# Mixing stages of a two-block network: rotation and turned blocks under the projection, gates by exponential and reciprocal

## The reference

```python
proj = n @ w_in                     # n: (256, 1024), normalised and modulated
# columns: NSA q, kv, gates (12); dilated q,k,v (6 heads); forgetting q,k,v (6 heads), f (6); merge gates (3*1024)
y_a = nsa(rope(q_a), rope(kc), vc, rope(ks), vs, rope(kw), vw, nsa_g, ...)   # compressed + 2 windows, 4 heads
# dilated: three groups of two heads; every group's own softmax and log-sum-exp
p, lse = masked_softmax(q k^T * scale);  out_g = p @ v
y_b = sum_g softmax_g(lse)[g] * out_g
# forgetting: cum = cumsum(log_sigmoid(f + bias)); scores + cum_q - cum_k, causal softmax
y_c = forgetting(fq, fk, fv, ...)
g_a, g_b, g_c = split(sigmoid(merge_g), 3)
merged = g_a * (y_a @ br_nsa) + g_b * (y_b @ br_dil) + g_c * (y_c @ br_fox)
h = h + gate * (merged @ w_out)
```

## Time and profile before

| | |
|---|---|
| runs (3) | median 2143.99 us, 2140.99 to 2145.86 |
| profiled execution | 2144.57 us, its span 2142.8 us |
| mean granted TensorE clock | 0.949 of full |
| busy: PE / DVE / ACT / POOL | 1964.4 / 1377.5 / 997.1 / 82.3 us |
| HBM read | 455.43 MB, 213 GB/s over the span |

### The profile page before, as it was taken

The page is one execution under the profiler, slowest core; times in us unless marked ns, Lnnn a source line. Parts: engine busy times, 40 slices in busy tenths (PEclk is TensorE's granted clock), DMA queues, the critical chain, the costliest instruction groups (busy, mean ns, idle before and its releaser), DMA issues.

```text
span 2142.8 us, 29870 instructions
## 1 busy us (share of the span) xinstructions
PE 1964.4 (92%) x12658; PEld 1746.6 (82%) x12658; DVE 1377.5 (64%) x1467; ACT 997.1 (47%) x1161; POOL 82.3 (4%) x105
## 2 busy tenths in 40 slices
PE   7999879999997999997997899999999879879998
PEld 3977668888885999896875799989998877768997
DVE  4888558999995777664335587777755443355444
ACT  3344337777774433443444433343334434435342
POOL 1320000000001000000000000000001000000000
PEclk9988979999998999997998999999999989989999
DMA  8655328999994687553321387658753432124554
GB/s 347 238 210 185 156 109 334 367 357 350 349 376 173 256 299 262 224 217 107 109 79 71 146 325 293 266 190 335 292 185 139 176 118 79 67 91 158 178 194 149
DMA packets 63877, 458.42 MB, mean 214 GB/s; under 512 B 7040, under 2 KB 7296, under 8 KB 8832
## 3 DMA queue, kind: packets, MB, share of 16 engines
q1 hardware_dynamic: 63744, 456.51, 56.7%
HBM read 455.43 MB, written 1.05 MB: 213 GB/s over the span
## 4 chain that ended last, share of the span: by engine, by line
issue 80%; PE 7%; DVE 6%; DMA 3%; ACT 2%; POOL 1%; DVEq 1%; POOLq 0%; ACTq 0%; SPq 0%
DMA ada<-in_ada 2%; DVE acc L326 2%; PE PS L353 2%; PE PS L354 2%; PE PS L355 1%; DVE wlo L280 1%; PE PS L1194 1%; POOL Z L485 1%; ACT whi L274 1%; DVE hlo L462 1%; PE PS L1258 1%; DMA raw<-in_stream 0%; ACT Z L441 0%; PE PS L1270 0%; DVE sm L1702 0%
## 5 line engine op out<-in xcount | busy, mean ns | idle before, releaser
L280 DVE TENSOR_TENSOR wlo<-raw,whi 128x2048 fp32r<-128x2048 f32 x282 | 646.6, 2294 | 409.1 <-ACT whi L274 403.6
L274 ACT ACTIVATE whi<-raw 128x2048 fp32r<-128x2048 f32 x282 | 538.5, 1913 | 408.4 <-PE PS L355 364.1
L353 PE MATMUL PS<-whi,hhi 128*128 128x256 f32 (+1 forms) x1616 | 530.2, 328 | 39.7 <-DVE wlo L280 11.7
L354 PE MATMUL PS<-wlo,hhi 128*128 128x256 f32 (+1 forms) x1616 | 518.5, 321 | 0.0
L355 PE MATMUL PS<-whi,hlo 128*128 128x256 f32 (+1 forms) x1616 | 518.0, 321 | 0.0
L353 PEld LDWEIGHTS PS<-whi,hhi 128*128 128x128 f32 x1616 | 319.9, 198 | 65.8 <-issue 13.7
L355 PEld LDWEIGHTS PS<-whi,hlo 128*128 128x128 f32 x1616 | 319.6, 198 | 19.2
L354 PEld LDWEIGHTS PS<-wlo,hhi 128*128 128x128 f32 x1616 | 320.3, 198 | 17.6
L353 PE MATMUL PS<-hhi,whi 128*128 128x256 f32 x1152 | 326.6, 284 | 2.2 <-DVE mod L348 2.2
L355 PE MATMUL PS<-hhi,wlo 128*128 128x256 f32 x1152 | 326.0, 283 | 0.0
L354 PE MATMUL PS<-hlo,whi 128*128 128x256 f32 x1152 | 326.0, 283 | 0.0
(11 more groups left out here) (377 smaller groups left out, 1822.0 us busy)
## 6 DMA issues: line engine op xcount, KB each, us to landing
raw<-in_stream SPq DMA_DIRECT2D x285, 1024.0 KB, 4.8
ada<-in_ada SPq DMA_DIRECT2D x92, 1024.0 KB, 4.9
ada<-in_stream SPq DMA_DIRECT2D x48, 1024.0 KB, 4.9
raw<-in_ada SPq DMA_DIRECT2D x3, 1024.0 KB, 15.5
xs<-in_x SPq DMA_DIRECT2D x1, 1024.0 KB, 11.7
Z<-in_ada SPq DMA_DIRECT2D x1, 1024.0 KB, 19.4
Z<-in_ctx SPq DMA_DIRECT2D x1, 1024.0 KB, 11.8
masks<-in_masks SPq DMA_DIRECT2D x2, 512.0 KB, 9.6
```

Of the source, the lines that this page charges most:

```text
L274: nc.scalar.activation(whi[:, s], src, ACT.Copy).then_inc(hi_ready, 1)
L280: nc.vector.tensor_tensor(wlo[:, s], src, whi[:, s].bitcast(F32), ALU.subtract).then_inc(lo_ready, 1)
L353: nc.tensor.matmul(out_, ah, bh, start=start, stop=False, skip_group_check=check)
L354: nc.tensor.matmul(out_, ah, bl, start=False, stop=False, skip_group_check=check)
```

## The change

Layer by layer in the mixing stage:

- Unit 11 of the projection (forget and NSA gate columns) streams and is projected first (`QKV_ORDER`). The forget logarithm starts on VectorE after unit 2 and ends after unit 4, the rotation follows after unit 5. The turned blocks go, in a new order with block 10 first, between projection units 7 to 11 (`TURNS_AT`).
- The running sums follow gate 0, their turns gate 1, and the compression gate 2. `oc_out` moves ahead of one `conv_lo`.
- The weights of the dilated groups come from row maxima and row sums: exp(m - max m) * sum instead of exp of m + ln(sum). They and the results of the dilated and first forgetting heads are made between the last maxima.
- Gates: sigmoid(x) becomes 1 / (1 + exp(-x)); the exponential on ScalarE (for gates 4 to 11 within the eviction), the addition and the reciprocal on VectorE (`gate_sigmoid`), between maxima of the passes; gate 11 after the passes.
- Results are turned in pairs of blocks as they become ready, beside gate 11; the third branch and the merged sum are handled in quarters. The products of the branches use other PSUM banks.

The diff, cut (`...` marks what is left out):

```diff
+QKV_ORDER = [11] + list(range(11))
+TURNS_AT = {7: (0, 4), 8: (4, 8), 9: (8, 12), 10: (12, 16), 11: (16, 17)}
...
-        ORDER2 = list(range(11, 17)) + list(range(11))
+        ORDER2 = [10, 8, 9, 6, 7, 0, 1, 2, 3, 4, 5] + list(range(11, 17))
...
-        ATT_GATES = {3 * (h // 2) + h % 2: (5 + h // 2, h % 2) for h in range(14)}
+        ATT_GATES = {3 * (h // 2) + h % 2: (5 + h // 2, h % 2) for h in range(12)}
...
             for j in range(3, 12):
                 pe.wait_ge(*B["q_out"].at(j - 3, l))
                 project(unit(pe, QK0 + j, E0), hhi, hlo, QB[j % 3]).then_inc(unit_used, 1)
...
+                if j == 7:
+                    pe.wait_ge(*B["rope2"].at(0, l))
+                    pe.wait_ge(*N2.row.at(1, l))
+                if j in TURNS_AT:
+                    pe.wait_ge(*B["q_out"].at(j - 1, l))
+                    turn_blocks(*TURNS_AT[j])
...
+                if i == PASSES2:
+                    pe.wait_ge(*B["y2_made"].at(0, l))
+                    turn_two(xn, 0, 6)
+            pe.wait_ge(*B["y2_made"].at(1, l))
+            turn_two(xn, 2, 4)
+            pe.wait_ge(*B["m_out"].at(10, l))
+            gate_unit(11, 7, 0)
+            pe.wait_ge(*B["y2_made"].at(2, l))
+            turn_two(xn, 4, 5)
+            gate_unit(11, 7, 1)
...
+                if f < 4:
+                    ins = nc.scalar.activation(G[f], src, ACT.Copy)
+                else:
+                    ins = nc.scalar.activation(G[f], src, ACT.Exp, scale=-1.0)
...
+                    if i < 4:
+                        nc.scalar.activation(G[i], G[i], ACT.Exp, scale=-1.0).then_inc(*B["gate_exp"].up)
...
-            for b in range(3):
-                for f in range(4 * b, 4 * b + 4):
-                    ins = nc.scalar.activation(G[f], G[f], ACT.Sigmoid)
-                ins.then_inc(*B["sig_done"].up)
...
             for j in range(12):
                 conv_lo(dve, QK0 + j + RING, E0)
+                if j == 2:
+                    fox_start()
+                if j == 4:
+                    fox_log()
+                if j == 5:
+                    rotate()
                 if l == 0 and 1 <= j <= 8:
...
+                if j in TURNS_AT:
+                    turned_out(*TURNS_AT[j])
...
+            def gate_sigmoid(f):
+                dve.wait_ge(*(B["gate_exp"] if f < 4 else B["m_out"]).at(f, l))
+                nc.vector.tensor_scalar(G[f], G[f], 1.0, None, ALU.add)
+                dve.drain()
+                nc.vector.reciprocal(G[f], G[f])
...
             for i in range(PASSES2):
                 dve.wait_ge(*B["s2_mm"].at(i, l))
...
                 if done[1]:
                     conv_lo(dve, CG[done[0]] + RING, E0)
+                    gate_sigmoid(done[0])
+                if i < 5:
+                    gate_sigmoid(i)
+                if i == 15:
+                    dil_weights()
+                if i == 18:
+                    dil_out()
+                if i == 19:
+                    fox_out(14, 2, 4, 256)
+            fox_out(16, 4, 5, 0)
```

More of the change, by code:

```diff
@@ L1837, in gate_unit, with turn_two @@
                     ins.then_inc(unit_used, 1)
-            gate_unit(0, 4)
[L1840 to L1853, removed]
+            pe.wait_ge(*B["tb_act"].at(7, l))
+            def turn_two(src, c0, bank):
+                for c in range(2):
+                    for t in range(NT):
+                        o = c * 256 + t * P
+                        ins = nc.tensor.transpose(PS[:, bank, o:o + P], src[:, t, (c0 + c) * P:(c0 + c + 1) * P], ident)
+                ins.then_inc(*B["y2_turned"].up)
+            gate_unit(0, 4)
             pe.wait_ge(*B["tb_dve"].at(7, l))
@@ L1955, in pe_layer @@
             pe.wait_ge(*B["br_out"].at(0, l))
[L1956 removed]
+            rows_product(u, 1, yb_hi[:, 3], yb_lo[:, 3], 0, True, False).then_inc(unit_used, 1)
             u = unit(pe, BR0 + 2, E0)
[L1958 to L1962, removed]
+            rows_product(u, 0, yb_hi[:, 4], yb_lo[:, 4], 0, False, False)
@@ new lines, in pe_layer @@
+            wh, wl = (w.rearrange("p (k n) -> p k n", k=2)[:, 1] for w in u)
+            for half in range(2):
+                for t in range(NT):
+                    o, w = slice(t * P, (t + 1) * P), slice(half * 512, half * 512 + 512)
+                    ins = mm3(PS[:, 2 * t + half], yb_hi[:, 5, o], yb_lo[:, 5, o], wh[:, w], wl[:, w], False, True)
+                ins.then_inc(*(unit_used, 1) if half else B["dil_mm"].up)
+            for j in range(4):
+                pe.wait_ge(*B["br_out"].at(2 + j, l))
+                turn_two(mg, 2 * j, 4 + j)
@@ L2287, in dve_layer @@
             dve.wait_ge(unit_used, E0 * 3 + (BR0 + 1))
-            branch(0, 4, mg)
+            for j in range(4):
+                ins = gated(0, j, 0, mg)
+            ins.then_inc(*B["br_out"].up)
             conv_lo(dve, BR0 + RING, E0)
             dve.wait_ge(*B["dil_mm"].at(0, l))
-            branch(1, 0, mt2[0])
-            conv_lo(dve, BR0 + 1 + RING, E0)
-            dve.wait_ge(unit_used, E0 * 3 + (BR0 + 3))
-            branch(2, 4, mt2[1])
-            conv_lo(dve, BR0 + 2 + RING, E0)
@@ L2296, in dve_layer, with merged @@
-            split_dve(dve, B["y2_hi"], B["y2_lo"], 3, 4, l)
+            for j in range(4):
+                gated(1, j, 4, mt2[0])
+            dve.drain()
+            nc.vector.tensor_tensor(mg, mg, mt2[0], ALU.add).then_inc(*B["br_out"].up)
+            dve.wait_ge(*B["dil_mm"].at(1, l))
+            def merged(j):
+                c = slice(256 * j, 256 * j + 256)
+                nc.vector.tensor_tensor(mg[:, :, c], mg[:, :, c], mt2[1][:, :, c], ALU.add).then_inc(*B["br_out"].up)
+            for j in range(2):
+                for t in range(NT):
+                    c = slice(256 * j, 256 * j + 256)
+                    nc.vector.tensor_tensor(mt2[1][:, t, c], PS[:, 2 * t, c], G[8 + j][:, t], ALU.mult)
@@ L2297, in dve_layer @@
+            dve.drain()
+            merged(0)
+            dve.wait_ge(unit_used, E0 * 3 + (BR0 + 3))
+            gated(2, 2, 0, mt2[1])
+            merged(1)
+            gated(2, 3, 0, mt2[1])
+            dve.drain()
+            merged(2)
+            merged(3)
+            for j in range(4):
+                split_lo(3 + j, 4 + j, hhi[:, 2 * j:2 * j + 2], hlo[:, 2 * j:2 * j + 2])
+            for u in range(1, 3):
+                conv_lo(dve, BR0 + u + RING, E0)
             conv_lo(dve, WO0 + RING, E0)
@@ L2510 @@
         gates = list(wide(m[:, fq + 1158:]))
-        seq += ffn[0] + list(wide(qkv)) + gates[:3] + [w1[:, :UNIT], w1[:, UNIT:]] + gates[3:]
+        seq += ffn[0] + [wide(qkv)[u] for u in QKV_ORDER] + gates[:3] + [w1[:, :UNIT], w1[:, UNIT:]] + gates[3:]
         seq += list(tall(branches)) + list(tall(a["mix_w_out_2"][l])) + ffn[1]
```

282 lines of the change are left out of this document (158 added, 124 removed).

## The result

The changed kernel takes 2155.8 us (median of 5 runs, 2153.5 to 2159.6), the kernel before beside it 2143.95 (5 runs, 2141.0 to 2145.9). The ratio is 1.0055, with a 95% interval of 1.0041 to 1.0070: slower by 0.55%, about 12 us. The prediction was 2156.

A forecast was written before the change was run, and what follows sets the result against it. TensorE, busy for 92% of the span, was taken as the bound, with VectorE's queue ahead of the maxima delaying it. Layer 0 at +9.6 and layer 1 at +1.5 made +11 on 2144.6, about 2156 us, range 2134 to 2182.

The forecast's parts named there:

- projection, layer 0: QKV projection of layer 0: 4.1 us of moved transposes, 4.9 of waits (rope2 2.9, evicted block 2.0), 3.4 of clock.
- front: Last projection unit to first attention mask: 42.5 us instead of 69.6, with no wait over 1.1 us left.
- attention: The 20 attention passes: 100.1 us grows by 26.4 from VectorE's queue and 8.5 from the clock, to 135.0.
- tail: Last attention pass to output projection: 32.5 us, a gain of 10.6 per layer, with gate 11 moved there.
- (3): Rival: a reciprocal takes 4.3 us, adding 22 us at 11 places per layer, 2178 us in all; chance 0.14.
- (4): Rival: long reciprocals stream better; about 2127 us at 2.0 us each, 2105 at the addition's cost; chance 0.16.
- the 22: Attention: each microsecond of reciprocal price changes the kernel's time by 22 us, from 11 places per layer on the path.
- the clock's 17 us: Attention, both layers: low clock behind TensorE's holes, charged at 1.7 us after each of five, 8.5 per layer.
- The walk: VectorE's queue stepped from the first mask through the attention passes, with 3.8 us per gate; sum +26.4 us.
- Anything VectorE gets between the two delays TensorE one for one: Attention: work put between conv_lo and the next maxima adds its full length to the 13.55 us period.
- Rival (2): TensorE's clock stays at 2.4 GHz through the holes, or its losses hide behind VectorE: 2136 to 2148 us; chance 0.15.
- Gate 11's two tiles leave: -6.0: Last attention passes: moving gate 11's two tiles to the tail takes 6.0 us per layer off the attention.

The follow-up runs named there:

- experiment 3: The changed kernel without its 24 wide reciprocals, each gate keeping its exponential and addition: 2084.6 us.
- experiment 6: The changed kernel with useless 128-column matmuls filling TensorE's holes ahead of its waits for exponentials: 2142.8 us.
- experiments 3 to 5: The changed kernel without wide reciprocals (2084.6 us), with them over half the columns (2122.1 us), and with additions and reciprocals moved to other places in VectorE's queue (2076.6 us).
- experiment 5: The changed kernel with 22 of VectorE's 24 gate additions and reciprocals moved to where VectorE waited, no instruction removed: 2076.6 us.
- experiment 8: The kernel of experiment 5 with the rotation ahead of conv_lo in the unit where VectorE waits for the late weight unit: 2074.5 us.
- 9: The kernel of experiment 8 with the nsa results behind pass 11, the dilated results behind pass 17, gates 7 and 8 one place later: 2070.1 us.
- 11: The kernel of experiment 2 with the rotation, the nsa and the dilated results at the places of experiment 8 and 9: 2074.0 us.
- 10: The kernel of 9 with VectorE's evictions ahead of the half steps and the first gated product ahead of the last gate unit's conv_lo: 2074.3 us.
- experiment 2: The changed kernel with the gates as before: plain evictions, twelve Sigmoids on ScalarE in the tail, no wide addition or reciprocal: 2075.1 us.

## Why the prediction was right

**Sign and size.** Slower by 11 was forecast, 12 measured. Most of its terms hold separately; two do not, and they partly cancel. The mechanism (work ahead of the maxima, holes in TensorE, low clock behind them) is what the runs show; that the sum came within 1 us is luck, as is part of the slope and of the clock's charge.

| term | forecast | measured |
|---|---|---|
| projection, layer 0 | +12.4 | +8.4 (69.5 for 61.15, first to last eviction) |
| projection, layer 1 | +4.1 | +3.5 (62.8 for 59.4) |
| front | 42.5 | 42.4 and 42.3 |
| attention | 135.0 | 138.5 and 136.9 |
| tail | 32.5 | 32.1 and 32.7 |
| whole mixing stage | +9.6, +1.5 | +8.6 (273.8 to 282.5), +3.5 (271.3 to 274.7) |

**The reciprocal.** The line through four short ones gave 3.3 us, the row says 3.353; the experiment's 1.753 at 256 columns lies on the same line (1.600 us for 256 columns, 6.25 ns each). Rivals (3) and (4) rested on other prices and fall with it; the time that each would have given can be read off the measured slope (21.1 and 21.4 for the 22 forecast; the sign turns at 3.35 - 11.9 / 21.2 = 2.8 us, as forecast). Only rival (4)'s 2105 for a reciprocal at the addition's cost does not follow from the 22: 2156 - 22 x 2.83 = 2094, and the measured slope gives 2096. The Trainium skill (VectorE: DVE Perf Modes, section Walkthrough: the 8-slice pipeline in each mode) says that reciprocal has a repeat count of eight; read as eight cycles per element at that page's clock, an estimate, it would have made some 4.3 us. The trace's 3.353 us does not agree with that reading.

**The slope.** Its size came out, its make-up did not. The 22 was eleven places per layer, one for one, with the clock charged apart. By these terms the kernel without reciprocals should have shed the clock's 17 us as well and come to 2156 - 74 - 17 = 2065; the 2082 expected in experiment 3 had kept the 17 in, and 2084.6 was measured. The measured 71 us from all to none hold the clock too, 13 us or so by experiment 6. What is left, 58 us for 3.353, is about 17 per microsecond, between eight and nine places per layer instead of eleven. The walk itself had that number: it adds 32.4 us for gates of 3.8, which is 8.5 of them. So 22 and 21.2 agree partly by luck.

**The queue.** "Anything VectorE gets between the two delays TensorE one for one" is shown for its place by experiments 3 to 5: straight response to the price, and full recovery by place alone. The walk through the first six passes forecast 47.7 us from the first mask to the reduce of pass 6; the row has 1067.59 - 1019.9 = 47.7. TensorE's waits came to 31.6 and 34.2 us, for "some 35", the longest 7.2 and 8.7 for "near 9". There are eight in each layer, but six holes of the size forecast (2.6 to 7.2 us in layer 0); the other two are 0.75 and 1.5 us, in layer 1 1.8 and 1.9, where the forecast's smallest was 2.4.

**The clock.** 8.5 us a layer charged, 7.9 and 5.5 taken away by filling the holes, which is a floor. Rival (2), no clock loss, falls: behind the holes the clock is at 0.50, and with most of the loss gone the kernel is at 2142.8. The charge's working does not hold, though. It took 3.5 us at the low level behind each of five holes; in layer 0 five stretches of 6.8 us stand at 0.50 (from 1047.1, 1067.6, 1088.1, 1108.6 and 1129.0). Over the attention of layer 0 TensorE is busy for 106.4 us, and for 92.6 in experiment 5 with the same instructions, 13.9 us more, of which filling the holes gave 7.9 back. And the low level does not halve the work: a gate's matmuls of 256 columns start every 0.213 us at 0.50 (1022.65 to 1026.49) and every 0.120 at 1.00 (1028.84 to 1031.36), a factor of 1.8. More low time than was charged, a part of it off the path, made nearly the number charged. The period of 17.3 us was forecast without the clock; measured it is 19.5, and with the holes filled 1089.05 - 1071.49 = 17.6.

**What was mis-sized.** Two terms, of opposite sign. "Gate 11's two tiles leave: -6.0" took the tiles' whole work off the path. They had been under waits, and putting them back lengthened the attention by 1.1 and -0.2 us; the credit was worth 1.1 us at most. With 5 more in that place, and 0.6 and 3.0 less for the clock, the 135.0 of each layer becomes 139.4 and 137.0, within 1 of the 138.5 and 136.9 that the stretches show. As the clock's figure is a floor, this does not prove the other terms one by one. In layer 0's projection the term of 12.4 was 4 too large: rope2's wait was 2.7 of 2.9, but the wait for the evicted block 0.2 instead of 2.0, and behind them came one low-clock stretch of 3.4 us, where I had charged for two. The smaller wait has a reason that experiment 8 shows: the two are one delay of VectorE's queue, so the first one pays for the second; I had added them. In layer 0 the attention's 3.5 too little and the projection's 4 too much cancelled, and the whole stage came out 1 us below the forecast; in layer 1, where the projection held, it came out 2 above. The sum is off by 1.

Not settled: whether the 4 us between the two forms of the gates (9 and 11), and the loss of 10 against 9, are real at this size; the intervals, 0.13% each way, touch.

## What to carry to other kernels

Look at what stands behind an instruction in its queue before pricing it: a gate's 3.8 us of VectorE work cost the kernel some 3.6 us ahead of the maxima (79 us for the 22 that moved) and nothing measurable behind them or in front of a wait. An engine that is 55% busy can be the bound, and its free places can be read from the idle times in the timeline. Work taken out of a wait gives nearly nothing back there and can cost its length where it goes (gate 11: at most 1 us back, some 5 spent); and two waits caused by one late queue are not to be added.

## What the hardware showed

- A RECIPROCAL is 0.15 us and 6.25 ns per column (3.353 us at 512 columns, 1.753 at 256), about eight times the addition of the same shape (0.42 us). The price per column is that of the short ones, which gave 6.1 ns from 2 to 24 columns.
- Behind the holes of the attention (up to 8.7 us) came stretches such as the 6.8 us shown at 0.50 of TensorE's clock; together they cost at least 7.9 and 5.5 us in the two layers; 90 matmuls of 128 columns (5.2 us) in each hole removed most of it (0.96 for 0.81).
- At 0.50 of its clock TensorE took 1.8 times as long for a matmul of 256 columns as at 1.00 (0.213 and 0.120 us from start to start), not twice.
- VectorE busy for 76 us instead of 36 beside the same TensorE work cost the attention at most 0.4 us in layer 0 and 2.0 in layer 1 (99.6 us each in experiment 5 for 99.2 and 97.6 in experiment 2).
